# A two-layer streaming encoder on one core: earlier table load, splits and bias row at the start, earlier splits and sums at the end

## The reference, cut to what matters

```python
lam = exp(sum(lam_q1 * lam_k1)) - exp(sum(lam_q2 * lam_k2)) + lam_init
bias = rel_bias_table[t5_bucket(k_pos - q_pos)]
x = x + (silu(h @ w_gate) * (h @ w_up)) @ w_down      # h = rmsnorm(x, g_ffn)
y = x * rsqrt(mean(x * x) + eps) * g_final
```

## Time and profile before

| | us |
|---|---|
| median of 3 runs | 1674.83 |
| the profiled execution, its own time | 1674.93 |
| its span | 1673.1 |
| TensorE busy (matmul) | 1640.5 |
| VectorE busy | 1106.3 |
| ScalarE busy | 805.0 |
| GpSimd busy | 578.5 |

### The profile page before, as it was taken

One profiled execution on the slowest core, in us unless ns is written; L12 is line 12 of the kernel. 1 busy time (PEld: TensorE's weight loads), 2 busy tenths in 40 slices (PEclk: granted clock), 3 DMA queues, 4 the chain that ended last, 5 costly groups with the idle time before them and its releaser, 6 DMA issues.

```text
span 1673.1 us, 31636 instructions
## 1 busy us (share of the span) xinstructions
PE 1640.5 (98%) x12236; PEld 1590.5 (95%) x12244; DVE 1106.3 (66%) x2058; ACT 805.0 (48%) x1506; POOL 578.5 (35%) x436
## 2 busy tenths in 40 slices
PE   9999999999999999999999999999999999999998
PEld 8989999999998999999999999899989999999998
DVE  5666655565656896587477689533458965874776
ACT  4465555454655654255144445545456541552443
POOL 4453446454454032022012357654550320220122
PEclk9999999999999999999999999999999999999999
DMA  7221223334323133233233322443241332332231
GB/s 188 80 60 57 60 76 97 73 101 103 87 63 80 52 101 114 64 101 102 76 88 90 82 72 69 114 109 93 63 116 52 101 102 70 98 110 77 76 96 64
DMA packets 282744, 145.45 MB, mean 87 GB/s; under 512 B 60334, under 2 KB 273004, under 8 KB 282596
## 3 DMA queue, kind: packets, MB, share of 16 engines
q1 hardware_dynamic: 278136, 136.27, 29.5%
q0 software_dynamic: 3616, 6.92, 1.6%
q10 hardware_dynamic: 844, 0.24, 0.1%
HBM read 130.69 MB, written 15.32 MB: 87 GB/s over the span
## 4 chain that ended last, share of the span: by engine, by line
PE 79%; DVE 12%; ACT 4%; issue 3%; DMA 1%; SPq 1%; POOL 0%; DVEq 0%; ACTq 0%
PE ACC L1286 37%; PE ACC L1699 7%; PE ACC L1701 7%; PE ACC L1700 7%; PE T L1286 3%; PE S L1286 2%; PE ACC L1566 2%; PE S L1541 2%; DVE SCO L2915 2%; DVE TOP L2912 1%; ACT PR L2142 1%; PE S L1701 1%; PE S L1699 1%; PE S L1700 1%; PE T L1554 1%
## 5 line engine op out<-in xcount | busy, mean ns | idle before, releaser
L3588 POOL TENSOR_TENSOR HF<-SG,U 128x576 f32<-128x576 f32 x44 | 65.1, 1479 | 498.2 <-ACT SG L2330 402.3
L1286 PE MATMUL ACC<-XGh,WH 128*128 128x288 f32 (+1 forms) x1008 | 227.7, 307 | 7.3 <-ACT U L2395 2.2
L3422 POOL TENSOR_TENSOR WL<-RAW,WH 128x1024 fp32r<-128x1024 f32 (+3 forms) x84 | 181.4, 2163 | 147.9 <-ACT WH L2017 147.6
L1286 PE MATMUL ACC<-XGh,WL 128*128 128x288 f32 (+1 forms) x1008 | 215.4, 295 | 0.0
L1286 PE MATMUL ACC<-XGl,WH 128*128 128x288 f32 (+1 forms) x1008 | 215.4, 295 | 0.0
L2017 ACT ACTIVATE WH<-RAW 128x1024 fp32r<-128x1024 f32 (+3 forms) x159 | 153.1, 971 | 82.0 <-PE ACC L1286 43.4
L1699 PE MATMUL ACC<-TB,WH 128*128 128x288 f32 x640 | 189.1, 295 | 0.6
L1701 PE MATMUL ACC<-TB,WL 128*128 128x288 f32 x640 | 188.8, 295 | 0.0
L1700 PE MATMUL ACC<-TB,WH 128*128 128x288 f32 x640 | 188.4, 294 | 0.0
L1286 PEld LDWEIGHTS ACC<-XGh,WH 128*128 128x128 f32 (+1 forms) x1008 | 159.2, 188 | 12.7 <-issue 3.5
L1286 PE MATMUL ACC<-HH,WH 128*128 128x288 f32 x960 | 166.5, 295 | 0.0
(11 more groups left out here) (473 smaller groups left out, 4390.0 us busy)
## 6 DMA issues: line engine op xcount, KB each, us to landing
RAW<-in_w_gate_dram SPq DMA_DIRECT2D x44, 512.0 KB, 3.9
RAW<-in_w_up_dram SPq DMA_DIRECT2D x44, 512.0 KB, 4.7
RAW<-in_w_down_dram SPq DMA_DIRECT2D x32, 512.0 KB, 4.1
RAW<-in_w_in_even_dram SPq DMA_DIRECT2D x29, 512.0 KB, 4.9
RAW<-in_w_in_odd_dram SPq DMA_DIRECT2D x28, 512.0 KB, 4.5
RAW<-in_w_out_even_dram SPq DMA_DIRECT2D x16, 512.0 KB, 4.2
RAW<-in_w_down_dram SPq DMA_DIRECT2D x16, 384.0 KB, 3.5
RAW<-in_w_out_odd_dram SPq DMA_DIRECT2D x8, 512.0 KB, 5.2
```

What stands on the lines that cost most here:

```text
L1286: ins = pe.matmul(out[0:m, 512 * b:512 * b + width], left, right[:, b * width:(b + 1) * width], start=(first and part == 0), stop=(last an ...
L3422: pool.tensor_tensor(WL[slot][:, 0:n], RAW[slot][:, 0:n], WH[slot][:, 0:n].bitcast(F32), ALU.subtract).then_inc(w_lo_pool, 1)
L3588: pool.tensor_tensor(HF[:, q, :], SG[:, q, :], U[:, q, :], ALU.mult).then_inc(h_out, 1)
```

## The change

It moves work and adds one instruction. At the start: ScalarE copies one column of ones into SEED once GpSimd has made them; it splits the unit of lat 3 between XGh 0 and the square of x 0 instead of behind the square; TensorE's second `keep_busy` has 12 products of ones instead of 14 (each shows as two matmul records), and the bias row's products come after tile 1, ahead of the turn of tile 4; GpSimd asks for the four lambdas when the square of tile 3 is there, ahead of adding it. At the end: the splits for tiles 6 and 7 both come at m = 4, ahead of tile 4's evacuation and square; and "sum 5" comes after three transposes of token tile 2 rather than after three of tile 2 and three of tile 3.

```diff
@@ tensor, start
-            keep_busy(14)
+            keep_busy(12)
...
                 if m == 1:
                     pe.wait_ge(c_in, 16 * 7)
                     out = open_pair("gv")
                     pe.transpose(out[0:P, 0:NG], GR[0:NG, :], IDN[0:NG, 0:NG]).then_inc(acc_done, 1)
-                if m == 2:
+                if m == 1:
                     pe.wait_ge(setup_c, 7)
                     pe.wait_ge(b_in, 16 * 2)
                     out = open_pair("vrow")
@@ tensor, end
             result_square_sums(4, SACC, 2, TOK_TILES).then_inc(acc_done, 1)
-            for t in (2, 3):
-                for m in range(4, DT - 1):
-                    turn_result(t, m)
+            for m in range(4, DT - 1):
+                turn_result(2, m)
             pe.wait_ge(sq_done, XFIN * 5)
             result_square_sums(5, SQ, 2, TOK_TILES).then_inc(acc_done, 1)
-            for t in (2, 3):
-                turn_result(t, DT - 1)
+            turn_result(2, DT - 1)
+            for m in range(4, DT):
+                turn_result(3, m)
@@ scalar, x_tile
                     act.activation(XGh[:, m, :], X[:, m, :], ACT.Copy, scale=GV[:, gcol + m:gcol + m + 1]).then_inc(xg_hi, 1)
                 n = XFIN * norm + m
+                if n == 0:
+                    unit_hi(("lat", KV_LATS[0]))
@@ scalar, start
+            act.wait_ge(setup_c, 1)
+            act.activation(SEED[:, :], ONES[:, 0:1], ACT.Copy)
             act.wait_ge(acc_free, acc.made("gain"))
             for m in range(DT):
                 x_tile(m, 0, GOFF[0], (x_taken, m + 1))
-                if m == 0:
-                    unit_hi(("lat", KV_LATS[0]))
@@ scalar and vector, ffn (the same lines in both)
-                        if m >= 2 and ("d", layer, part, m) in splits:
+                        if m >= 2 and ("d", layer, part, m) in splits and not in_stretches(layer, part, m):
                             begin("d", layer, part, m)
+                        if in_stretches(layer, part, m) and m == LAST_ROWS[0]:
+                            begin("d", layer, part, m)
+                            begin("d", layer, part, m + 1)
@@ gpsimd
+            def load_lambdas():
+
+                for i, lam in enumerate(("lambda_q1", "lambda_k1", "lambda_q2", "lambda_k2")):
+                    pool.dma_start(LV[:, i, :], bass.AP(a[lam].tensor, 0, [[0, P], [1, DIFF_DIM]])).then_inc(lam_in, 16)
+
             def add_squares(norm):
...
+                    if n == 3:
+                        load_lambdas()
                     if m == 0:
...
             pool.dma_start(OH[:, :], a["onehot"]).then_inc(b_in, 16)
-            for i, lam in enumerate(("lambda_q1", "lambda_k1", "lambda_q2", "lambda_k2")):
-                pool.dma_start(LV[:, i, :], bass.AP(a[lam].tensor, 0, [[0, P], [1, DIFF_DIM]])).then_inc(lam_in, 16)
             add_squares(0)
```

## The result

The changed kernel takes **1678.63 us** (median of 16 runs, 1675.36 to 1680.93). The kernel before, run beside it, takes 1674.92 (16 runs, 1673.67 to 1675.88). The ratio is 1.0021, interval 1.0014 to 1.0027: slower by 0.2%, where 1674.7 was forecast and no change held to be nearly certain. The median lies 2.1 us above the range's upper end of 1676.5.

What follows compares the result with a forecast made beforehand. TensorE was taken as the bound, busy 1640.5 of 1673.1 us. Start +0.87, end -0.69 and -0.33 sum to -0.15 us, giving a median of 1674.7, range 1672.9 to 1676.5; same speed at 0.94.

Steps and rivals of the forecast that it cites:

- XGl 1: Start, VectorE: low weights that the next products wait for, to end at 14.15 instead of 15.41.
- lat 4: Start: TensorE opens it at 22.45 instead of 21.58, 0.87 us later, because GpSimd's add holds VectorE's split.
- the forecast's order: Start: GpSimd's add of tile 3 comes after VectorE's XGl 3 and ahead of its split of lat 4, holding that split.
- one end wait gone and SQ's sum sooner: End: tile 7's early split removes a wait, 0.69 us; "sum 5" passing three transposes gains 0.33 us.
- the first products: Start, TensorE: to come at 11.9, 1.5 us sooner, from earlier low weights and four fewer records of ones.
- XGh 0: Start, ScalarE: to come at about 8.50, 1.26 us sooner, with the table load hidden in idle time.
- The hold of the split: Start: GpSimd's add of tile 3 holds VectorE's split of lat 4 for about 1.25 us.
- From there TensorE is packed: Behind the opening of lat 4: TensorE has no slack, so the 0.87 us shift stays to the end.
- rival C: Start: TensorE's idle 2 us near 20.4 to 22.4 costs its rate, 2.5 us lost, giving 1677.2; chance 0.03.
- Rival B: Start: the add comes before 18.4, holds XGl 3; the next add holds the split; lat 4 2.3 us late, 1676.1; chance 0.15.
- Rival A: Start: the add comes behind 19.2, VectorE's split goes first, lat 4 opens 0.43 us sooner, 1673.4; chance 0.25.
- the rule that stood beside rival A: VectorE can lock GpSimd out of the memory it writes descriptors into, so requests beside a busy VectorE stretch.

Runs made afterwards that it cites:

- again: The changed kernel, unedited, run in the first set for another trace: 1677.91 us, ratio 1.0007 to the kernel before.
- slowA: Changed kernel; GpSimd's add of tile 3 waits for XGl 3, VectorE's split of lat 4 waits for that add: 1676.92 us, ratio 1.0017 to before.
- again2: The changed kernel, unedited, run once more: 1678.14 us, ratio 1.0021 to the kernel before.
- busy17: Changed kernel with 17 products of ones instead of 12 in the wait for x part 2: 1677.15 us, ratio 1.0009 to before.
- fill: Changed kernel with 9 unread products of ones in TensorE's wait ahead of lat 4: 1675.57 us, ratio 1.0000 to before.
- after: The changed kernel's first profiled execution, the least of its 16 runs: 1675.36 us, span 1673.6.
- dveorder: Changed kernel, VectorE splitting lat 4 and reading vrow ahead of taking x tile 4: 1674.89 us, ratio 0.9998 to before.
- portwait: Changed kernel, GpSimd's add of tile 3 waiting until VectorE has split lat 4: 1673.89 us, ratio 0.9995 to before.
- lamearly: Changed kernel with the lambdas asked for at the start again, ahead of GpSimd's first add: 1674.35 us, ratio 0.9992 to before.
- forceA: Changed kernel, GpSimd's add of tile 3 waiting for VectorE's XGl 3: 1673.54 us, ratio 0.9996 to before.
- slowAfill: slowA with 9 products of ones ahead of tile 3's products, where TensorE would wait: 1676.01 us, ratio 1.0010 to before.
- the fourth set: The last set of experiments, with slowA, slowAfill and again2; the kernel before measured 1674.16 us there.
- forceAfill: forceA with 9 products of ones ahead of tile 3's products: 1674.77 us, ratio 1.0003 to before.
- best: Changed kernel, VectorE splitting lat 4 and reading vrow ahead of x tile 4, GpSimd's add of tile 3 behind XGl 3: 1673.44 us, ratio 0.9990.
- lamlate: The kernel before with the late request of the lambdas alone: 1674.26 us, ratio 0.9994 to before.

## Why the prediction was wrong

**Right, by its own steps.** The table load at 4.31 in idle time; the bias row's products at 15.73 (15.75 forecast); tile 4 turned at 16.89 (16.9); XGl 1 ended at 14.04 (14.15); lat 4 at 22.64 (22.45) in the execution that follows the forecast's order; one end wait gone and SQ's sum sooner, 1.01 us together (1.02). Two small steps missed without effect: the first products came at 12.41 and not 11.9, since x part 2 was waited for (1.12 us), a wait that the step left out; and XGh 0 came at 7.68, another 0.8 us sooner, because the first turn of x began at 5.88 here and took 0.63 us, against 6.29 and 1.02 before. The hold of the split was put at 1.25 us and is 1.46. The lambdas landed 5 us behind their requests, not 7.4.

**The step that failed** is the one sentence "From there TensorE is packed, and everything else is tied to it, so the shift stays to the end", and with it rival C at a chance of 0.03. TensorE's wait of 2.3 us was seen and was forecast to 0.3 us. What it does was not. Seven traces have a wait of 1.7 us or more near 20 to 24 us, and in five of them the granted clock fell to 0.50: in again and slowA just behind the wait, in again2, busy17 and fill within it. In after (2.26 us) and dveorder (1.92) it did not. The pace lost is 1.3 (busy17), 1.5 (again, slowA) and 2.2 us (again2).

The reason given for 0.03 was that the shorter waits of the trace cost no pace. That is true of the one execution that was traced. The waits of 0.8 us at lat 4 in portwait, lamearly and forceA cost none either. But the wait of 1.17 us near 542, which stands in that trace too, costs 1.4 to 2.0 us in six others: one trace without a loss was no argument, neither about a wait of 2.3 us nor about a shorter one.

Rival C priced 2.5 us where 1.3 to 2.2 were lost. Its sum of 1677.2 comes near the measured 1678.63 in part by luck: it has neither the later opening of rival B nor the loss near 545 in it. Counted over executions, the unedited kernel reached a mean clock of 0.999 in 4 of 39, the kernel before in 83 of 130 in the four sets. The count is coarse. One stretch at half pace costs the mean about 0.001, wherever it lies, and the idle end of the execution lowers it too: before's profile has no such stretch until 1665 us, 0.50 from 1670 on, and stands at 0.999.

The Trainium skill, "TensorE: Matmul & The Clock Gate", section "Part 1: The HAM clock gate (the "warmup" mystery)", says that how many products of one kernel run at the lower level at its start varies from run to run. The traces agree: the same 24 products of ones took 5.49 us in before and 4.61 in after.

**Rival B was underpriced in chance (0.15), not in size.** It opens lat 4 2.43 us late in again2, where 2.3 was worked out. Its condition was wrong: the add was to come ahead of XGl 3's start, put at 18.4, "0.1 us below my window" of 18.5 to 19.0. In again2 the add comes 0.14 us behind that start, in fill 0.54, and it goes first in both. What differs is how far the requests have come: XGl 3 begins 1.26 to 1.33 us behind the first of them in after, again and busy17, before the last request, and 2.06 and 1.66 behind it in again2 and fill, beside the last one. Both ends move: the first request began between 16.39 and 17.21 in these five, XGl 3 between 17.65 and 18.87. I had taken one execution's times as fixed where they move by 0.8 us against each other. How many of the executions run by B is open: it stands in two of the five traces that have the changed kernel's own order and late lambdas (again2 and fill, not after, again and busy17).

**Rival A's condition was met and A did not happen.** In the profile of after the add came behind 19.2, at 19.34, and still won; in again (18.59) and busy17 (19.27) too it came behind the start of the split, and won. With one wait on GpSimd between the requests and the add, A is real: forceA 1673.54 and portwait 1673.89, where 1673.4 was worked out.

So the change costs a late opening (+1.1 in after, +2.4 where the add meets XGl 3) and the pace lost behind it (1.3 to 2.2 us), and gains 1.0 at the end. In the traces the loss near 545 comes on top (us; the sum takes -1.0 for the end, as measured in after):

| trace | lat 4 opens, against 21.58 | pace lost near 22 | pace lost near 545 | sum | span, against 1673.1 |
|---|---|---|---|---|---|
| after | +1.1 | 0 | 0 | +0.1 | +0.5 |
| again | +0.3 | 1.5 | 1.5 | +2.3 | +1.6 |
| busy17 | +1.0 | 1.3 | 2.0 | +3.3 | +3.1 |
| slowA | +0.8 | 1.5 | 1.4 | +2.7 | +3.0 |
| again2 | +2.4 | 2.2 | 0 | +3.6 | +3.2 |
| slowAfill | +2.2 | 0 | 0 | +1.2 | +1.6 |

The sums meet the spans within 0.7 us. The forecast's order with the pace lost near 22 alone gives +1.6 (1.1 + 1.5 - 1.0), so a typical execution needs rival B's opening or the loss near 545 besides; which of the two how often is open. In the fourth set the parts stand as medians: again2 +4.0, slowA without the tie +2.8, slowAfill without the tie and the lost pace +1.9, of which the filler's own delays may be a part. The last does not come down to the forecast's -0.15; its fastest run is 0.7 above that of before. Why the profiled execution of after kept its clock is open.

## What to carry to other kernels

A wait that is forecast to grow from nothing to 2 us on a saturated TensorE is priced with the pace behind it, not as its length; that a wait cost none in one trace says little, since the wait near 542 cost none in eleven traces and 1.4 to 2.0 us in six. Where the instructions of two engines can hold each other up, ask how far each one's start moves from run to run, and where the answer decides, order them with a semaphore: one wait on GpSimd, for whose adds nothing on the path waited, was worth 4 us here. And one profile is one execution: read its time against the others before its steps are taken for all.

## What the runs showed of the hardware

- **An add right behind a request goes first.** Of two instructions with two operands in SBUF, one on VectorE and GpSimd's add right behind its last request, VectorE's started first by 0.11 us (dveorder, 19.47 against 19.58), 0.14 (again2), 0.15 (after), 0.18 (busy17), 0.21 (again) and 0.54 (fill, 18.87 against 19.41), and GpSimd's went first each time. All six of VectorE's began while the last request ran. Where the add waited for a semaphore behind its requests, VectorE's went first with no more of a lead: 0.16 in forceA (18.57 against 18.73), 0.17 in forceAfill (18.47 against 18.64). So did slowA's split, 0.11 ahead of the add of tile 4 (20.34 against 20.45). In best XGl 3 began beside the last request (19.21), the add waited, and XGl 3 took its 0.80. So the lead in the start times does not decide; why an add behind a request has its turn so early is open. The Trainium skill, "SBUF — State Buffer", section "Who interferes with whom", says that the issue order decides who blocks; the starts that these traces show don't follow that order in the six.
- **A waiting engine is next.** With both waiting the turn alternates: in again2 and in fill the add of tile 3, XGl 3, the add of tile 4, the split. That is how one late add holds two of VectorE's instructions.
- **Requests on GpSimd aren't held by such instructions.** One ran at 18.59 in 0.54 us in lamlate, beside VectorE's split of 18.10 to 19.32; in the idle start of before the first took 0.56. The same section infers this: `tensor_tensor` needs only the read side, writing descriptors the write side. So the rule that stood beside rival A in the prediction does not show with these instructions.
- **The clock's drop is not certain, and not only at lat 4.** The same wait of 1.17 us near 542 us is followed by 18 products in 2.46 us in eleven traces and by the same 18 in 3.9 to 4.5 us in six. The kernel before has runs of up to 1681.8 us at a mean clock of 0.994 or 0.995.
